# First norm of a two-block transformer kernel: half of the squares on VectorE, half of the features turned between the blocks of the first matmul group

## The reference

```python
def rms_norm(x, g):
    xf = x.astype(jnp.float32)
    y = xf * lax.rsqrt(jnp.mean(xf * xf, axis=-1, keepdims=True) + RMS_EPS)
    return (y * g.astype(jnp.float32)).astype(x.dtype)
# first block: h = rms_norm(x, norm1_g); h @ w_in, of whose columns 1536 feed the Hyena branch
u = short_conv(u, conv_w, conv_b)          # three taps along the tokens
# hyena_filters: a small network with two sines, then a product with w3, a decay and an FFT
h = jnp.sin(f1.astype(f32) * (z @ w1.astype(f32) + b1.astype(f32)))
h = jnp.sin(f2.astype(f32) * (h @ w2.astype(f32) + b2.astype(f32)))
h = (h @ w3.astype(f32)).reshape(L, HY_ORDER, HY_DIRS, HY_WIDTH)
h = h * decay[:, None, None, :]
```

## Time and profile before

| | us |
|---|---|
| median of 3 runs | 1688.45 |
| lowest, highest | 1688.43, 1689.16 |
| profiled execution | 1687.88 |
| its span from first to last instruction | 1686.1 |
| TensorE busy in the span | 1626.7 |
| ScalarE busy, VectorE busy | 644.0, 876.7 |

### The profile page before, as it was taken

The page is one execution under the profiler, slowest core; times in us unless marked ns, Lnnn a source line. Parts: engine busy times, 40 slices in busy tenths (PEclk is TensorE's granted clock), DMA queues, the critical chain, the costliest instruction groups (busy, mean ns, idle before and its releaser), DMA issues.

```text
span 1686.1 us, 19261 instructions
## 1 busy us (share of the span) xinstructions
PE 1626.7 (96%) x7582; PEld 1286.9 (76%) x7582; DVE 876.7 (52%) x1401; ACT 644.0 (38%) x1106; POOL 338.7 (20%) x286
## 2 busy tenths in 40 slices
PE   5999998988999999999999999999999999999998
PEld 4566787766767788888888887786788888888886
DVE  5446555367457555434442324477564677777222
ACT  4332223355445433332332222366553444444222
POOL 3443205364012116111110205011103300000000
PEclk9999999999999999999999999999999999999999
DMA  6211112211221323232223332321102223222322
GB/s 233 63 63 40 48 55 85 80 62 51 74 65 50 113 88 100 88 100 99 89 99 101 99 90 78 104 63 51 51 2 87 89 89 98 93 95 88 125 91 72
DMA packets 39222, 139.52 MB, mean 83 GB/s; under 512 B 4331, under 2 KB 4971, under 8 KB 38940
## 3 DMA queue, kind: packets, MB, share of 16 engines
q1 hardware_dynamic: 39132, 138.29, 25.2%
HBM read 136.14 MB, written 2.10 MB: 82 GB/s over the span
## 4 chain that ended last, share of the span: by engine, by line
PE 84%; DVE 6%; POOL 4%; ACT 3%; issue 2%; DMA 1%; SPq 0%; POOLq 0%; DVEq 0%; ACTq 0%
PE ps L387 81%; PE ps L390 3%; POOL sqs L2101 2%; POOL sqt L2099 1%; DVE raw L1056 1%; DVE wlo L863 1%; ACT whi L1482 0%; DVE T L1089 0%; DMA wraw<-in_ws 0%; DVE tp L1051 0%; DMA x<-in_x 0%; DVE sd L962 0%; DVE raw L1043 0%; ACT tp L1601 0%; DVE st L1095 0%
## 5 line engine op out<-in xcount | busy, mean ns | idle before, releaser
L863 DVE TENSOR_TENSOR wlo<-wraw,whi 128x1024 fp32r<-128x1024 f32 (+2 forms) x220 | 271.7, 1239 | 441.5 <-ACT whi L1482 440.9
L387 PE MATMUL ps<-hThi,whi 128*128 128x512 f32 x1128 | 453.4, 402 | 1.7 <-DVE skT L1387 0.9
L387 PE MATMUL ps<-hThi,wlo 128*128 128x512 f32 x1128 | 439.7, 390 | 0.0
L387 PE MATMUL ps<-hTlo,whi 128*128 128x512 f32 x1128 | 439.4, 390 | 0.0
L1482 ACT ACTIVATE whi<-wraw 128x1024 fp32r<-128x1024 f32 (+2 forms) x244 | 252.0, 1037 | 479.3 <-PE ps L387 465.2
L387 PEld LDWEIGHTS ps<-hThi,whi 128*128 128x128 f32 x1128 | 211.9, 188 | 57.5 <-issue 16.2
L387 PEld LDWEIGHTS ps<-hTlo,whi 128*128 128x128 f32 x1128 | 212.1, 188 | 45.0 <-issue 3.6
L387 PEld LDWEIGHTS ps<-hThi,wlo 128*128 128x128 f32 x1128 | 211.8, 188 | 44.9
L387 PE MATMUL ps<-whi,hThi 128*128 128x512 f32 (+1 forms) x224 | 90.2, 402 | 6.8 <-DVE wlo L863 6.8
L387 PE MATMUL ps<-wlo,hThi 128*128 128x512 f32 (+1 forms) x224 | 85.3, 381 | 0.0
L387 PE MATMUL ps<-whi,hTlo 128*128 128x512 f32 (+1 forms) x224 | 85.3, 381 | 0.0
(11 more groups left out here) (322 smaller groups left out, 2564.2 us busy)
## 6 DMA issues: line engine op xcount, KB each, us to landing
wraw<-in_ws SPq DMA_DIRECT2D x236, 512.0 KB, 3.5
x<-in_x SPq DMA_DIRECT2D x4, 512.0 KB, 6.7
x<-in_x SPq DMA_DIRECT2D x1, 2048.0 KB, 8.5
out<-ys SPq DMA_DIRECT2D x8, 256.0 KB, 2.2
dec<-in_dec SPq DMA_DIRECT2D x1, 1024.0 KB, 14.6
wraw<-in_ws SPq DMA_DIRECT2D x4, 256.0 KB, 2.6
vec<-in_vec SPq DMA_DIRECT2D x1, 788.0 KB, 4.8
w<-in_w SPq DMA_DIRECT2D x1, 512.0 KB, 12.8
```

What stands on the lines that cost most here:

```text
L387: return t.matmul(o, l, r, start=first, stop=last)
L863: v.tensor_tensor(wlo[h][:, 0:width(i)], wraw[h][:, 0:width(i)], whi[h][:, 0:width(i)].bitcast(F32), ALU.subtract).then_inc(lo_done[h], 1)
```

## The change

Four things are changed. (1) The squares: ScalarE keeps features 0 to 511 of each slice and VectorE takes features 512 to 1023 with a multiply-and-sum instruction (its order: slices 0, 1, scale 0, slice 2, scale 1, slice 3, scales 2 and 3). (2) TensorE turns the first three slices of strips 0 to 3 as each slice is scaled, then the fourth slice of each; the group `hy0` begins with these four strips. (3) Strips 4 to 7 become four steps of a new generator `norm_rest` ahead of `filters`, with banks 4 to 7. (4) `hy0` runs with rate 3 in place of 2: a step after block 1, after block 2 and after block 3. It has 12 steps: four strips, one with which the generator ends, and seven of `filters`.

```diff
+        def turned(j, i):
+            w.wait_ge(n_row, i + 1)
+            return across(4 + j % 4, i, x1[:, i, j * 128:(j + 1) * 128])
+        def norm():
+            for i in range(3):
+                for j in range(4):
+                    turned(j, i)
+            for j in range(4):
+                turned(j, 3).then_inc(n_tr, 1)
+                free[4 + j] = [(n_lo, j + 1)]
+        def norm_rest():
+            for j in range(4, 8):
+                take(j)
                 for i in range(4):
-                    w.wait_ge(n_row, i + 1)
-                    op = across(bank, i, src[:, i, k * 128:(k + 1) * 128])
+                    op = turned(j, i)
                 op.then_inc(n_tr, 1)
+                free[j] = [(n_lo, j + 1)]
+                yield
...
-        norm(x1)
-        flow.beside += [filters(), hyena()]
+        norm()
+        flow.beside += [norm_rest(), filters(), hyena()]
         for g in range(3):
-            group("hy%d" % g, hT, h_ready(0), lambda b: (cv_v, 2 * (4 * g + b) + 2), 2)
+            group("hy%d" % g, hT, h_ready(0), lambda b: (cv_v, 2 * (4 * g + b) + 2), 3 if g == 0 else 2)
...
+        def squares(i):
+            w.wait_ge(in_x[i], 16)
+            if i:
+                w.wait_ge(n_sv, i)
+            r = x1[:, i, 512:1024]
+            v.tensor_tensor_reduce(junk1[1][:], r, r, 1.0, 0.0, ALU.mult, ALU.add, small[:, 49 + 2 * i:50 + 2 * i]).then_inc(n_sv, 1)
+        def normed(k):
+            w.wait_ge(n_hi, k + 1)
+            v.scalar_tensor_tensor(hTlo[:, k, :], ps[4 + k % 4][:], col("g1", k), hThi[:, k, :].bitcast(F32), ALU.mult,
+                                   ALU.subtract).then_inc(n_lo, 1)
...
-        for i in range(4):
-            scaled(i)
+        squares(0)
+        for i in range(1, 4):
+            squares(i)
+            scaled(i - 1)
+        scaled(3)
         split(LA)
-        norm()
+        for k in range(4):
+            normed(k)
...
-            w.wait_ge(n_sq, 2 * i + 2)
+            w.wait_ge(n_sv, i + 1)
```

More of the change, by code:

```diff
@@ L187, in build @@
     zT = sb("zT", AR + 126, [33, S])
-    junk1 = sb("junk1", AR, [128, 512])
+    junk1 = [sb(f"junk1_{i}", AR + 2 * i, [128, 512]) for i in range(2)]
     w3 = sb("w3", AR + 88, [64, 4, 512])
@@ L296, in build @@
     blocks = sem("blocks")
-    n_sq, n_rs, n_row, n_tr, n_hi, n_lo = (sem(n) for n in ("n_sq", "n_rs", "n_row", "n_tr", "n_hi", "n_lo"))
+    n_sq, n_sv, n_rs, n_row, n_tr, n_hi, n_lo = (
+        sem(n) for n in ("n_sq", "n_sv", "n_rs", "n_row", "n_tr", "n_hi", "n_lo"))
     f_mlp, f_sin, f_h, f_ws, f_gen, f_td, f_sq, f_acc, f_dft, f_et, f_cc, f_nrm, f_nv, f_np, l_v, l_e = (
@@ L874, in scaled, with norm_rest @@
             v.tensor_scalar(x1[:, i, :], x1[:, i, :], small[:, 8 + i:9 + i], None, ALU.mult).then_inc(n_row, 1)
[L876 to L880, removed]
+        def squares(i):
[8 more added lines that the diff above has]
+                                   ALU.subtract).then_inc(n_lo, 1)
+        def norm_rest():
+            for k in range(4, 8):
+                normed(k)
+                yield
         def means(n, bank):
@@ L1391, in vector_program @@
         w.wait_ge(in_vec, 16)
-        for i in range(4):
-            scaled(i)
+        squares(0)
[3 more added lines that the diff above has]
+        scaled(3)
         split(LA)
-        norm()
-        flow.beside += [filters(), hyena()]
+        for k in range(4):
+            normed(k)
+        flow.beside += [norm_rest(), filters(), hyena()]
         for g in range(3):
-            group("hy%d" % g, conv(g), 2)
+            group("hy%d" % g, conv(g), 3 if g == 0 else 2)
         for half in range(2):
@@ L1454, in first_half @@
             w.wait_ge(in_late, 48)
-            w.wait_ge(n_sq, 8 + b + 1)
+            w.wait_ge(n_sq, 4 + b + 1)
             v.tensor_tensor(y0[:, b, :], p[:], fg[:, 0:512], ALU.mult).then_inc(w_y, 1)
@@ L1459, in second_half @@
         def second_half(b, p, done):
-            w.wait_ge(n_sq, 12 + b + 1)
+            w.wait_ge(n_sq, 8 + b + 1)
             w.wait_ge(n_rs, 12 + b + 1)
@@ L1488, in group, with squares, normed, norm_rest @@
                     evac(b, ps[BANK[name] + b], DONE[name] + b + 1)
[L1490 to L1499, removed]
+        def squares(i):
+            if i:
+                w.wait_ge(n_sq, i)
+            a.activation(junk1[0][:], x1[:, i, 0:512], ACT.Square, accum_out=small[:, 48 + 2 * i:49 + 2 * i]).then_inc(n_sq, 1)
+        def normed(k):
+            w.wait_ge(n_tr, k + 1)
+            a.activation(hThi[:, k, :], ps[4 + k % 4][:], ACT.Copy, scale=col("g1", k)).then_inc(n_hi, 1)
+        def norm_rest():
+            for k in range(4, 8):
+                normed(k)
+                yield
         def filters():
@@ L1873, in scalar_program @@
             w.wait_ge(in_x[i], 16)
-            for half in range(2):
-                squares(i, half)
+            squares(i)
         split(LA)
-        norm()
-        flow.beside += [filters(), hyena()]
+        for k in range(4):
+            normed(k)
+        flow.beside += [norm_rest(), filters(), hyena()]
         for g in range(3):
-            group("hy%d" % g, conv(g), 2)
+            group("hy%d" % g, conv(g), 3 if g == 0 else 2)
         for half in range(2):
@@ L1930, in last_squares @@
             w.wait_ge(blocks, done)
-            w.wait_ge(n_sq, 8 + q)
+            w.wait_ge(n_sq, 4 + q)
             c = 48 + 2 * b + half
@@ L1963, in roots @@
             q, c = 3 * i, 48 + 2 * i
-            w.wait_ge(n_sq, 2 * i + 1)
+            w.wait_ge(n_sq, i + 1)
             g.tensor_scalar(small[:, i:i + 1], small[:, c:c + 1], 1.0 / D, EPS, ALU.mult, ALU.add).then_inc(n_rs, 1)
-            w.wait_ge(n_sq, 2 * i + 2)
+            w.wait_ge(n_sv, i + 1)
             w.wait_ge(n_rs, q + 1)
@@ L2162, in fox, with norm_rest @@
             flow.later(1, lambda: out_norm_scale(7))
+        def norm_rest():
+            for _ in range(4):
+                yield
         none = lambda b: None
@@ L2174, in gpsimd_program @@
         split(LA)
-        flow.beside += [filters(), hyena()]
+        flow.beside += [norm_rest(), filters(), hyena()]
         for i in range(3):
-            group("hy%d" % i, none, 2)
+            group("hy%d" % i, none, 3 if i == 0 else 2)
         for half in range(2):
```

4 lines of the change are left out of this document (removed).

## The result

| us | before | after |
|---|---|---|
| median of the runs, of 6 each | 1688.81 | 1702.38 |
| profiled execution | 1687.88 | 1697.69 |
| its span | 1686.1 | 1695.9 |

The change makes the kernel slower: ratio 1.0071, 95% interval 1.0059 to 1.0083, about 12 us. One run of after at 2112.79 us was disturbed: it isn't in the ratio, but it is in the median of the table, which is 1701.92 without it. The direction was predicted; the size was not: 6.6 us and 1695.0 were forecast, with a range of 1691.0 to 1697.5. The profiled executions differ by 9.8, and the other four runs of after took 1700.70 to 1703.54. The profiled execution is the fastest of its kernel, so it shows less than the median has lost.

A forecast was written before the change was run, and what follows sets the result against it. TensorE, busy 96% of the span, was taken to bound the kernel. A start of 0 plus new waits of 1.0 + 4.2 + 1.4 = 6.6 us on 1688.45 gave 1695.0 us, range 1691.0 to 1697.5.

The forecast's parts named there:

- The start: Squares, scaling and turning until all strips are turned: 0 us net, bounds 1.7 gained and 1.0 lost.
- the price of the roots: GpSimd's roots between scalings: 1.26 us each plus about 0.5 held, ends at 10.5, 12.1, 13.7, 15.3.
- The transposes inside `hy0`: Sixteen transposes moved between the blocks: 1.7 us, plus 0.4 for changes between transposes and matmuls.
- The first wait: TensorE ahead of the first w product, for sums behind a sine held by GpSimd's subtraction: 1.0 us.
- The second wait: TensorE ahead of the second w product, for the bank that the first fs empties: 4.2 us.
- The third wait: TensorE ahead of the third w product, for the next fs: 1.4 us.
- Later parts: Behind the fourth w product, each step one step later in the groups: taken as 0, no place above 0.3 us.
- The sum: Whole kernel: 0 at the start plus 1.0 + 4.2 + 1.4 = 6.6 us of new waits, nothing given back.
- The scaling escapes the subtraction: Fourth scaling not held by GpSimd: start gains 1.7, new waits stay, +4.9 us, 1693.3; chance 0.08.
- the sine isn't held up: Second sine free of GpSimd's subtraction, first wait 0, start gains 0.8: 4.5 us more, 1693.0; chance 0.1.
- Contention is worse: Start loses 1.0 and the sine is held 0.9 us more: +8.5 us, 1697.0; chance 0.08.
- The delay is absorbed later: Later TensorE waits on something running on its own time swallow the 6.6 us: 1686.8 to 1688.5; chance 0.12.

The follow-up runs named there:

- after_again: The changed kernel, unaltered, run and profiled once more; median 1703.31 us, ratio 1.0072 to the kernel before.
- e7_pool_waits: The kernel before, with GpSimd starting its first weight subtraction only when the fourth slice is scaled; 1687.85 us, ratio 0.9991.
- e5_taps_later: The changed kernel with VectorE's taps of hy0 done behind block 3, so the first fs stands ahead of them; 1693.73 us, ratio 1.0022.
- e4_filled: The changed kernel with 16 unused matmuls ahead of the second w product, to keep TensorE busy; 1698.94 us, ratio 1.0055.
- e9_shift: The kernel before with one empty step ahead of the filter steps, nothing else; 1691.98 us, ratio 1.0020.
- e2_turning: The changed kernel with all squares on ScalarE again; strips, steps and rate 3 stay; 1701.15 us, ratio 1.0067.
- e10_taps_pool: The changed kernel with VectorE's taps behind block 3 and GpSimd's first subtraction waiting for the fourth scaling; 1690.20 us, ratio 1.0010.
- e8_mixed_pool: The changed kernel with squares on ScalarE, filter steps mixed with strips, and GpSimd waiting for the fourth scaling; 1690.18 us, ratio 1.0005.
- e6_mixed: The changed kernel with all squares on ScalarE and filter steps taken in turn with the four strips; 1692.04 us, ratio 1.0012.

## Why the prediction was right in direction and too small

**The start.** Predicted 0, within 1.7 gained and 1.0 lost; measured 0.9 lost. The h product is at 42.09 against 32.78, and 36 more matmuls stand ahead of it, 8.41 by the earlier trace rows: 42.09 - 32.78 - 8.41 = 0.9. In after_again, where the low pace ended three matmuls sooner, it is at 41.86, 0.7 lost. The step that was off is the price of the roots. The prediction let a scaling hold one of the three root instructions, 1.6 us a root; the trace has two held, one by the scaling and one by the next square, and 2.15 from scaling to scaling. (The 1.6 was also short of the prediction's own terms, 1.26 and a hold of 0.5. It had the hold by the square as its worse end, at 0.5 on each of two slices; that measured 0.23, and the hold by the scaling 0.56 on each of three roots.) So the fourth scaling starts at 16.67 and not at 15.3, and the first matmul at 21.68 and not at 20.2. That the scaling is held for 2.82 again, and that the earlier matmuls run at the low pace (0.43), came as predicted. The transposes inside `hy0` cost less than the 2.1 they were priced at, 1.8 (each four of them put 0.44 between two matmuls), which hides a part of the 1.5 us by which the first matmul is late. The Trainium skill (SBUF — State Buffer, section SBUF: two separate sides) says that the port pair that VectorE and GpSimd share is locked for a whole instruction, and that who starts first has it. The traces agree in both directions: 0.75 for a root instruction of 0.19, and 2.82 for a scaling of 0.75, which e7_pool_waits brings back to 0.75.

**The first wait.** Predicted 1.0, measured 1.06. The held sine instruction is there, 1.71 (44.03).

**The second wait.** Predicted 4.2, measured 4.01, released by `fs`, which stands behind the four taps. e5_taps_later, which moves only them, removes it.

**The third wait.** Predicted 1.4, measured none. Here the prediction failed. It took the matmuls behind a wait at the pace of the earlier trace rows. After idling 4.01 us, TensorE ran at its lower clock. One block and one product took 6.38 from 57.44 to 63.82, where e5_taps_later shows 3.49 for them without a wait: 2.9 us. `fs` was ready in that time, so the 1.4 was hidden beneath it and only 1.5 is a net loss in this execution. In e4_filled, where the clock stayed up, the forecast wait is there, 1.18. In the execution of after_again the lower clock lasted until about 72: from the second w product to the fourth it took 15.65 (57.21 to 72.86), where 3.49, the 1.4 and 4.90 make 9.8, a net loss of 5.9 that the forecast has at 0. The prediction had the rule in hand: it priced the lower clock at the start, from the transposes, and did not ask what the clock would do behind the wait of 4.2 us that it forecast 35 us later. The Trainium skill (TensorE: Matmul & The Clock Gate, section HAM oscillation — how this bites in real kernels) describes a kernel that loses time in this way, by waits between bursts of matmuls that send the clock down again. The window of after (0.53) and that of e4_filled (1.00) agree.

**Later parts.** Predicted 0, with the remark that each step stands one step later. This term too was put too low. e9_shift, which makes that shift alone, shows 1.2 us of idle time at W and `sd` from 64 to 500 us, and both traces of after have the same two waits, 1.9 and 1.1. In the profiled executions of after and before, 8.7 of the 9.8 us are reached at the product of `fs` with `cu`: it is at 73.48 against 61.82, and 12 more matmuls stand ahead of it, 2.94 from 48.94 to 51.88 in the trace of before. That leaves 1.1 behind it, the size of what the shift costs. It is a remainder and not a reading: other waits between 64 and 500 us differ as much from trace to trace (those of the transposes for `st` are 2.4 in after and 1.2 in after_again).

**The sum.** In the profiled execution: 0.9 + 1.06 + 4.01 + 2.9 = 8.9 up to that product, for which its place says 8.7, and 1.1 later. That makes 10.0 by the terms, for 9.8 measured. The forecast was 6.6. Of the 3.2 that are missing, 0.9 is the start, 1.5 the clock behind the second wait, and 1.1 the shift; the two waits together are 0.1 smaller, and 0.2 are within the rounding of these readings.

The forecast was for the median, and by it the loss is 12 us (ratio) to 13.1 (1701.92 against 1688.81). The execution of after_again stands nearer to it, with a span 15.4 above that of before: 0.7 at the start, 1.06 and 4.01 for the waits, 3.1 and 4.2 for the low clock behind the second, 13.1 in all, for which the place of the product of `fs` with `cu` says 12.9, and 2.5 behind it, of which the shift explains about half; the rest stays open. So the largest error of the forecast is the clock behind its own second wait. That most executions have the lower clock for longer is shown for the one that was profiled (after_again); for the others it rests on their mean clock.

**The rivals.** "The scaling escapes the subtraction" is refuted by the fourth scaling, 2.82 again, and "the sine isn't held up" by its instruction of 1.71. "Contention is worse" was near for the start, 0.9 where it had 1.0, though with other terms: the scaling ended later than it had it, at 19.49 and not at 19.1, and the transposes were cheaper. It was wrong for the sine. "The delay is absorbed later" is refuted: none of it came back, and 1.1 to 2.5 us are added behind the first 74 to 78.

**What stays open.** Ten of the twelve traces have the wait of 1.39 or 1.40 for the sine. Behind it the clock fell in four of them (e2_turning, e5_taps_later, e9_shift, e10_taps_pool) and not in the other six; in e8_mixed_pool, which has no such wait, it fell behind the one of 1.25 ahead of the first w product (0.57 granted from 46 to 50 us). Whether that belongs to these kernels or to the execution wasn't tried; a second profile of one of them would be needed. It moves a result by 1.6 us, as much as the difference between e5_taps_later and e6_mixed.

## What to carry to other kernels

A wait of a few us on TensorE can cost more than its length: here 4.01 us brought 1.5 to 5.9 more. Ask of every wait that is forecast what the granted clock will be behind it, and price the next stretch at either level. When steps are moved in a fixed order, look at which engine's evacuation lands ahead of a producer that others wait for; here four taps in front of one `fs` made two thirds of the loss, and the cure was to move VectorE's taps, not the matmuls. To shorten a chain, see who holds its instructions before giving one of them to another engine: one added line, a wait on GpSimd, gained 1.8 us, where splitting the squares gained nothing.

## What the runs showed of the hardware

- The clock's lower level lasts for very different times behind the same wait: about 7 us in one execution of after (the w product of 3.78 at 57.44, full pace at 63.82) and at least 15 in the other (57 to 72 at 0.50). TensorE was busy from the end of the wait on in both, with w products of 64 rows and blocks of 128 rows in turn.
- Behind the same wait of 1.39 us the clock was at 0.50 and 0.57 in e9_shift and e10_taps_pool, and full in the kernel before.
- VectorE's square with two equal SBUF inputs, 0.69 long, is not held by GpSimd's one-column instructions, but holds them: 0.50 and 0.51 in place of 0.27.
- A wait that keeps GpSimd's 128x1024 subtraction off one VectorE instruction shortens it from 2.82 to 0.75, and the subtraction loses nothing that TensorE would notice in the kernel before.
- At the start the granted clock reads 1.00 in after from 21 to 26 us and in before from 18 to 24, while the matmuls of after start 0.43 apart until 25.66 and 0.23 apart behind it. There the pace has to be read from the steps between the starts.
